# Constant multiplications ahead of and between the first transposes of a hybrid decoder step

## The reference, cut to what matters

```python
xn = rmsnorm(h, g_norm)      # 528 prompt rows + 8 sample rows, each of 2048 values
proj = xn @ w_in             # w_in: 2048 x (2*1024 + 768 + 512 + 64 + 1024)
```

## Time and profile before

| | us |
|---|---|
| median of 3 runs | 1095.8 |
| lowest, highest | 1095.18, 1104.16 |
| profiled execution, its own time | 1097.7 |
| its span from first to last instruction | 1095.6 |
| TensorE busy in the span | 1032.9 (94%) |
| VectorE, ScalarE busy | 623.2 (57%), 378.9 (35%) |

### The profile page before, as it was taken

One profiled execution on the slowest core, in us unless ns is written; L12 is line 12 of the kernel. 1 busy time (PEld: TensorE's weight loads), 2 busy tenths in 40 slices (PEclk: granted clock), 3 DMA queues, 4 the chain that ended last, 5 costly groups with the idle time before them and its releaser, 6 DMA issues.

```text
span 1095.6 us, 26948 instructions
## 1 busy us (share of the span) xinstructions
PE 1032.9 (94%) x10653; PEld 954.6 (87%) x10653; DVE 623.2 (57%) x1337; ACT 378.9 (35%) x797; POOL 157.6 (14%) x257
## 2 busy tenths in 40 slices
PE   5999999999999999999999999788988899999995
PEld 5999999999999999988899987565655479999995
DVE  4685535451585655678785436688888633234332
ACT  6621111211233312144651231544554413233233
POOL 0002410000130000010322512323434100000000
PEclk9999999999999999999999999889999999999998
DMA  9548643323363443265545756859999893322313
GB/s 259 121 132 151 162 107 97 84 63 98 100 168 104 108 133 96 68 153 174 152 142 154 232 179 213 264 156 280 287 282 292 226 321 104 110 78 77 86 29 156
DMA packets 201773, 169.80 MB, mean 155 GB/s; under 512 B 37548, under 2 KB 166055, under 8 KB 200103
## 3 DMA queue, kind: packets, MB, share of 16 engines
q1 hardware_dynamic: 178566, 119.12, 39.3%
q0 software_dynamic: 11616, 29.06, 8.9%
q10 hardware_dynamic: 11496, 20.32, 5.2%
HBM read 140.84 MB, written 25.26 MB: 152 GB/s over the span
## 4 chain that ended last, share of the span: by engine, by line
PE 78%; ACT 5%; SPq 5%; DVE 4%; issue 4%; DMA 3%; POOL 1%; ACTq 0%; DVEq 0%; POOLq 0%
PE gemm L2138 14%; PE gemm L2139 13%; PE gemm L2140 13%; PE gemm L2506 6%; PE gemm L2508 6%; PE gemm L2507 6%; PE misc L2410 2%; PE gemm L2425 2%; PE gemm L2455 2%; PE misc L2165 1%; PE gemm L2344 1%; SPq L518 1%; PE gemm L2346 1%; PE gemm L2345 1%; PE misc L2224 1%
## 5 line engine op out<-in xcount | busy, mean ns | idle before, releaser
L2138 PE MATMUL gemm<-xh,w_hi 128*128 128x260 f32 (+2 forms) x1056 | 301.8, 286 | 0.2 <-DVE ev L1392 0.2
L2139 PE MATMUL gemm<-xl,w_hi 128*128 128x260 f32 (+2 forms) x1056 | 299.9, 284 | 0.0
L2140 PE MATMUL gemm<-xh,w_lo 128*128 128x260 f32 (+2 forms) x1056 | 299.4, 284 | 0.0
L865 ACT ACTIVATE w_hi<-w_raw 128x2048 fp32r<-128x2048 f32 (+3 forms) x63 | 90.7, 1439 | 316.0 <-PE gemm L2140 278.5
L2138 PEld LDWEIGHTS gemm<-xh,w_hi 128*128 128x128 f32 x1056 | 198.7, 188 | 1.0 <-issue 0.4
L2140 PEld LDWEIGHTS gemm<-xh,w_lo 128*128 128x128 f32 x1056 | 199.2, 189 | 0.0
L2139 PEld LDWEIGHTS gemm<-xl,w_hi 128*128 128x128 f32 x1056 | 199.0, 188 | 0.0
L1324 DVE TENSOR_TENSOR w_lo<-w_raw,w_hi 128x2048 fp32r<-128x2048 f32 (+3 forms) x63 | 109.9, 1745 | 156.0 <-ACT w_hi L865 153.8
L2506 PE MATMUL gemm<-comb_hi,w_hi 128*128 128x260 f32 x512 | 147.7, 288 | 1.2 <-DVE comb_lo L2000 1.1
L2507 PE MATMUL gemm<-comb_lo,w_hi 128*128 128x260 f32 x512 | 145.4, 284 | 0.0
L2508 PE MATMUL gemm<-comb_hi,w_lo 128*128 128x260 f32 x512 | 145.4, 284 | 0.0
(11 more groups left out here) (399 smaller groups left out, 1978.2 us busy)
## 6 DMA issues: line engine op xcount, KB each, us to landing
w_raw<-w_in SPq DMA_DIRECT2D x35, 1024.0 KB, 6.7
ckv<-cache_ckv POOLq DMA_DIRECT2D x76, 256.0 KB, 4.0
w_raw<-w_out SPq DMA_DIRECT2D x16, 1024.0 KB, 5.8
ckv<-cache_ckv SPq DMA_DIRECT2D x52, 256.0 KB, 3.6
z_d<-ev ACTq DMA_DIRECT2D x16, 260.0 KB, 2.1
w_raw<-w_glu SPq DMA_DIRECT2D x8, 512.0 KB, 4.6
yt<-x_prompt SPq DMA_DIRECT2D x4, 1024.0 KB
o_y_p<-yt SPq DMA_DIRECT2D x4, 1024.0 KB
```

What stands on the lines that cost most here:

```text
L865: act.activation(w_hi[:, slot, 0:width], w_raw[:, slot, 0:width], ACT.Copy).then_inc(w_hi_ready, 1)
L2138: pe.matmul(acc, a, xa, start=k == 0, stop=False)
L2139: pe.matmul(acc, a, xb, start=False, stop=False)
L2140: last = pe.matmul(acc, b, xa, start=False, stop=k == k_tiles - 1)
```

## The change

A helper `keep_running(count)` issues `count` multiplications of the 128x128 identity by the 128x128 `ones`, both float32, into 128 columns of `gemm[2]`. They wait for nothing and signal nothing, and what they leave in the bank is overwritten by `first_half(1, 1, 0, ...)`. Fourteen stand ahead of the first four groups, three ahead of groups 4 and 5, three ahead of groups 6 and 7, eight ahead of the first product. The call `turn_x(range(0, 8))` is cut into three to make room.

```diff
-            turn_x(range(0, 8))
+            def keep_running(count):
+                for _ in range(count):
+                    pe.matmul(gemm[2][:, 0:P], ident[:], ones[:], start=True, stop=True)
+
+            keep_running(14)
+            turn_x(range(0, 4))
+            keep_running(3)
+            turn_x(range(4, 6))
+            keep_running(3)
+            turn_x(range(6, 8))
+            keep_running(8)
             pe.wait_ge(gemm_read, 2)
             pe.wait_ge(w_lo_ready, 1)
             first_half(0, 0, 0, range(KD), KD)
```

## The result

The changed kernel is slower: 1105.13 us, the median of 22 runs (1099.92 to 1112.21), against 1095.68 for 22 runs of before (1089.32 to 1104.16). The ratio is 1.0083, with a 95% interval of 1.0066 to 1.0101. I had said 1095.7, with a range up to 1098.8. Of the 9.4 us lost, the profiled execution shows 4.4 (span 1100.0 against 1095.6).

A forecast was written before the change was run, and what follows sets the result against it. TensorE, busy 94% of the span, bounds the kernel; the prologue's end ties with block 2's load. TensorE gains 0.9 us but waits until 52.45, so nothing arrives: span 1095.6, median 1095.7 us, range 1093.8 to 1098.8.

The forecast's parts named there:

- the first premise: The change touches only the first 18 us, so the timeline was read there and along the waits to about 52 us.
- the last: Behind the prologue, TensorE, busy for 94% of the span, carries an early or late shift along.
- All five cases: The predicted outcome and its four rivals for the whole kernel, all between 1094.3 and 1098.5 us.
- Price of one added multiplication, and the fourteen: Program start: 0.28 us per multiplication at the upper clock, 0.52 at the lower; the fourteen end at 8.8 us.
- The slow stretch goes: First products, 18.64 to 22.00 us: with the last pause filled the clock stays up, giving 1.47 us back.
- The gain does not reach the end: End of prologue: TensorE waits for weight block 2 until 52.45, so of 0.9 us nothing arrives; chance 0.66.
- Rival B: End of prologue: block 2's load is not last, so 0.9 to 1.4 us arrive, 1094.3 to 1094.9; chance 0.12.
- TensorE leaves the prologue 0.9 us early: Block 1's first product 0.9 us earlier, at 24.2, carried to the small transposes, which end at 51.4 instead of 52.27.
- Nothing in this path waits for TensorE: Load of weight block 2: its start, at about 41.0 us, does not depend on TensorE.
- Rival C: Prologue: the fourteen hold up the transposes of x, slower, 1096.6 up to 1098.5 or so; chance 0.10.
- Rival E: Prologue: filling does not keep the clock up, or it falls elsewhere; 1095.8 to 1096.5; chance 0.05.
- Rival D: Behind the new pause of about 1.1 us at 51.4, the clock falls and costs 1.5 us: 1097.2; chance 0.07.

The follow-up runs named there:

- e1: Changed kernel with each of the 28 added multiplications cut to 32 columns by 32, same 112 added instructions; 1108.15 us, ratio 1.0108.
- e5: Kernel before with 28 small multiplications (112 instructions) directly ahead of the paging stage's loop; 1104.96 us, ratio 1.0088.
- e13: Kernel before with 28 small multiplications (112 instructions) in the middle of the paging stage, ahead of tile 16 of 32; 1107.03 us, ratio 1.0093.
- e4: Kernel before with 28 small multiplications (112 instructions) behind the paging stage, at the start of the output projection; 1098.29 us, ratio 1.0011.
- e2: Changed kernel with 36 more small multiplications (144 instructions) ahead of the fourteen, 256 added instructions in all; 1098.18 us, ratio 1.0016.
- e14: Kernel before with 28 small multiplications directly ahead of the paging stage and 36 more ahead of tile 16, 256 instructions in all; 1100.91 us, ratio 1.0028.
- e15: Kernel before with 64 small multiplications (256 instructions) directly ahead of the paging stage; 1099.22 us, ratio 1.0023.
- e6: Kernel before with the change's eight multiplications ahead of the first product and 56 small ones ahead of the first transposes, 256 instructions; 1098.02 us, ratio 1.0017.
- e3: Kernel before with 64 small multiplications (256 instructions) ahead of the first transposes; 1097.71 us, ratio 1.0004.
- e9: Of the change only the eight multiplications ahead of the first product (32 instructions), no padding; 1106.25 us, ratio 1.0096.
- e7: Kernel before with 32 small multiplications (128 instructions) ahead of the first transposes; 1107.31 us, ratio 1.0093.
- e8: Kernel before with 16 small multiplications (64 instructions) ahead of the first transposes; 1107.42 us, ratio 1.0111.
- e10: Kernel before with 60 small multiplications (240 instructions) ahead of the first transposes; 1104.32 us, ratio 1.0050.
- e12: Kernel before with 56 small multiplications (224 instructions) ahead of the first transposes; 1102.84 us, ratio 1.0057.
- e11: Kernel before with 4 small multiplications (16 instructions) ahead of the first transposes; 1103.52 us, ratio 1.0062.

## Why the prediction was wrong

**The step that failed** is the first premise, "the change touches only the first 18 us", and the last, that behind 52.45 TensorE carries its shift along unchanged. All five cases took the later stages as they were. The change moved every later instruction by 112 places in the blocks in which TensorE's instructions arrive. That costs 9 us in the paging stage (e1, e5, e13), costs nothing measurable in the output projection (e4), and is undone by 144 instructions more (e2). From 53 to 690 us the changed kernel stays 0.1 to 1.2 us behind. None of the rivals held it, and a "slower" chance of 0.01 was far too sure for an unrolled program that I had read only to 53 us.

**Price of one added multiplication, and the fourteen**: the sum came out, by luck. The 28 instructions of the fourteen took 6.1 us (2.95 to 9.05), forecast 5.8. But I had counted 4 us at 0.52 us per multiplication and the rest at 0.28. In the trace all 28 instructions are issued at one slow pace, 0.21 us apart, 0.43 per multiplication, and the quick pace begins only at 9.05 with the transposes; the eight then take 0.22 per multiplication (16 instructions, 0.11 apart). Both prices were too high, and the quick part of the fourteen did not exist. ScalarE started at 9.75, forecast 9.5. The first product came at 18.53, forecast 18.2.

**The slow stretch goes**: it did, but not shown to be by the filling. The granted clock of the changed kernel is 1.00 from 19 to 22 us. The prediction took the slow stretch of one execution for a trait of the kernel. Of the six traces whose start is that of before, two have the fall (18.7 in before, 18.6 in e13). In e4 and e5 the clock came up only at 16.9 and 16.5, behind all 32 transposes, and did not fall; in e14 and e15 it came up at 20.8 and 20.5.

**The gain does not reach the end**: right, and shown apart from the rest by the pauses of e4 and e5 above, and by e2 and e6, both level with before. Rival B, the gain coming through, has nothing for it: the intervals of e2 and e6 begin at 0.9993 and 0.9994, and 1.0 to 1.5 us would be 0.9986 to 0.9991. Both carry 256 added instructions, but so does e3, without the clock's gain, and it is level with them; what e2 and e6 do not have is the early load of before.

**TensorE leaves the prologue 0.9 us early**: too much. The small transposes end at 51.77, 0.50 before the 52.27 of the earlier trace rows; ScalarE's delay was 0.69 (9.75 against 9.06), not 0.4. Nothing hung on it.

**"Nothing in this path waits for TensorE"** for the load of block 2: right by the letter, but the load starts 1.0 us later in the changed kernel, which is twice the 0.5 us that I had named as a sign of being wrong. Here too it is the place of TensorE's packets that changed; see the last section. It costs 0.64 us at 53 us, and what is left of that at the end cannot be told.

**Rival C**, the fourteen holding up the rows of x: not the cause, e9 has none of them and is as slow. **Rival E**, the filling not keeping the clock up: did not happen in this trace. **Rival D**, the clock falling at the new wait: did not happen in the changed kernel, at a pause of 1.32 us, but it did in e6, e7, e8, e10 and e12, at pauses of 2.5 to 3.2 us. A window of the changed kernel behind the wait:

```profile
53.20:55.00 1.80, 1.80 (x16) 1.80 (x17) 0.00 (x0) 1.57 (x1) 0.00 (x0) 1.00 0.82 200
```

**How a boundary costs**, as far as it can be read. In the changed kernel the packet starts at 806.7 us and the product behind the boundary at 809.09; in e13 it is 808.7 and 811.31. In before the two longest pauses are 1.73 and 1.29 us, with packets at 846.4 and 801.6 and products at 848.9 and 804.1. In these four it is 2.4 to 2.6 us from the start of a packet to the end of the pause, and 2.2 to 2.9 in all 73. What TensorE still has in its queue can hide a part. Ahead of the pause of 2.5 us it has just been through 96 products of `page_scores` in about 1.5 us (the rows above), and so it has ahead of that of 2.8 in e13; little is left to hide them. This reading is argued from the rows, not tested by itself.

The pauses alone do not make the loss. Those at boundaries add to 4.4 us in before (four of them), 6.5 in the changed kernel and 7.4 in e1 (five in each), for spans 4.4 and 10.0 us longer; in e2, which lost nothing, they add to 5.9. What differs first is where they stand. In every displaced kernel that is slow a boundary pause of 1.7 us or more falls behind the dense run of `page_scores`: in `scores` (the change, e1, e5, e8, e13) or at its own last products, L2431 of before (e7, e9, e10, e11, e12). Waits of e12 and e9, where that line is L2436 and L2438:

```profile
PE gemm L2436 <- issue: 4.3, 2, 3.7
```

```profile
PE gemm L2438 <- issue: 4.0, 3, 2.0
```

In before, e2, e3, e4, e6 and e15, all level or nearly so, no "issue" wait stands at either place, and in e14 one of 0.3 us. ScalarE and VectorE wait for the scores, and GpSimd's page loads for `weigh_pages` behind them, which frees their buffers. From 800 to 900 us those last waits are, of before and then of the changed kernel:

```profile
POOL ckv L474 <- PE gemm L2455: 27.1, 10, 4.7
```

```profile
POOL ckv L474 <- PE gemm L2465: 34.8, 11, 4.7
```

**What follows a pause** is the second part. The product behind the pause takes 0.59 us in e13 and e8, against 0.29 in before. The granted clock had fallen. In e13 it is 0.50 from 810.5 to 820.7 us, in the changed kernel from 811.1 to 814.5. Window of e13, with the ten products of `weigh_values` that stand there and the first behind them:

```profile
811.00:820.00 9.00, 8.01 (x21) 3.68 (x21) 3.71 (x7) 1.47 (x6) 2.15 (x4) 0.50 0.64 209
```

```profile
815.23 5.49 PE L2410 MATMUL misc<-pt,vraw 128*128 128x512 f32 x10 [0.68 <-issue]
820.64 0.46 PE L2443 MATMUL misc<-prt,ident 128*32 128x32 f32 x32
```

The same products in before:

```profile
808.04 2.88 PE L2410 MATMUL misc<-pt,vraw 128*128 128x512 f32 x10 [0.71 <-issue]
810.86 0.46 PE L2443 MATMUL misc<-prt,ident 128*32 128x32 f32 x32
```

From the third product of `scores` to L2443 it is 9.33 us in e13 and 5.27 in before. So the pause of 2.84 us is followed by 4.06 us lost to the slow clock. In the changed kernel the pause costs 2.6 us and the stretch at 0.50 behind it 1.4. Between 740 and 885 us the granted clock is 0.50 for 17 us in e13, 14 in e1, e8 and e10, 7 in e5, e11 and e12, 3 in the changed kernel and e7, none in e9; and for none in before, e4 and e14, 3 in e2, e6 and e15, but 14 in e3, which is level. The means over whole executions point the same way: the median granted clock is 0.978 in the 22 runs of the changed kernel and 0.977 to 0.981 in e1, e5 and e7 to e13, against 0.982 or 0.983 for before in every group and 0.982 to 0.985 in e2, e4, e6, e14 and e15 (e3: 0.980). By an estimate from these, 0.004 of 1100 us is 4.4 us of clock time, about half of the loss.

**Shown** is that the position of TensorE's instructions modulo 256 in the second half of the paging stage makes the loss. The place of the pauses goes with it in every trace, but no kernel here moved one boundary alone, so that it is their cause is argued. That the clock falls behind the long pauses and makes them dearer is read from the traces, the e13 rows above all, and was not varied by itself; e3 shows that such stretches need not cost at the end. **Open** is the rest of the way from pauses of 2 to 4 us to a loss of 5 to 12, and single traces say little on sizes: e9's profiled execution had a span of 1096.2, against a median time of 1106.25, and the highest clock of its seven (0.986), while e6's was the slowest of its twelve (1102.8).

## What to carry to other kernels

An instruction added to a long unrolled program is not local: it shifts all later instructions of its engine in their 16 KB blocks, and where short matrix instructions run on a busy DMA system, a boundary in the wrong place can cost microseconds, by its pause and by the stretch at the lower clock behind it. Before pricing such an edit, look for "issue" pauses in unrolled stages, and at the granted clock behind them; to measure what an edit is worth in itself, pad it to a whole number of 256 instructions, as e2 and e6 do, and look at what the padding itself moves: there it made the load of block 2 1.9 and 2.3 us late. And a gain ahead of a transfer that is on the chain of waits should be checked against that chain first: here the quicker products only made TensorE wait longer. And a slow stretch in one trace should be looked for in a second trace of the same code before an edit is made against it: with an untouched start it was there in two of six.

## What the runs showed of the hardware that was not expected

- Time against the number of added TensorE instructions comes back at 256: level with before at 256 (e2, e3, e6), and 5 to 12 us above it (by the ratios) at the seven numbers tried between. Nothing beyond 256 was tried.
- From the start of an instruction packet to the end of the pause it was 2.2 to 2.9 us in 73 pauses, and TensorE stood still for up to 3.7 us at such a boundary (e12).
- Behind a pause of TensorE in the paging stage the granted clock can be 0.50 for 3.4 to 10.2 us; in e13 that took 4.06 us on top of a pause of 2.84.
- When the clock first comes up, and whether it falls again, differed between executions of the same start: up at 11.9 us and 0.50 from 18.7 to 22.1 (before), up at 16.9 and no fall (e4), up at 20.8 (e14). The clock column of a window has 1.00 also ahead of the first of these changes, where the trace has no record of the clock; there the pace tells the level, as the 421 ns of the earlier trace rows.
- Instructions added at the very start also move a load that no TensorE instruction holds up. The load of block 2 started at 40.6 to 41.2 us in the six traces with an untouched start, at 41.32 with 16 instructions added there (e11), at 42.00 in the changed kernel, and at 43.27 in e6. It goes with where TensorE's packets fall among SyncE's issues. In the changed kernel one packet starts at 22.1 us in place of 26.5, in the midst of one long issue. Timelines of SyncE, before and after:

```profile
18.70 7.57 SPq L508 DMA_DIRECT2D bbar<-ssm_b_im  x1
```

```profile
18.55 8.49 SPq L508 DMA_DIRECT2D bbar<-ssm_b_im  x1
```

  This issue took 8.4 to 8.7 us in the five traces with a packet between 21 and 25 us (the change, e1, e7, e8, e9) and 7.1 to 7.8 in the other twelve. In the same way the issue at L495 took 6.4 to 6.7 us in the five with a packet at 10 us (e2, e3, e6, e10, e12), and 5.1 to 5.3 in the others. No run was made to test it.
- Small multiplications have a slow and a quick pace too. The 128 products of e3 (64 calls) stand 53 ns apart at the start, and the 16 of the same kind ahead of e1's first product of block 0, with the clock up, 33 ns apart (timelines of e3 and of e1):

```profile
2.95 6.36 PE L2098 MATMUL gemm<-ones,ident 128*32 128x32 f32 x128
```

```profile
15.11 0.69 PE L2098 MATMUL gemm<-ones,ident 128*32 128x32 f32 x16
```

  The 32 products of `spread_page_weights` (L2443, shown above), 0.46 us in all, are quicker still, 14 ns apiece. They write to four groups of partitions in turn, and `small` always to the same; whether that is the reason was not tested.
